# Two short runs of dummy matmuls taken out of a decoder layer on one core

## The reference

```
f1 = swiglu(rms_norm(x, ffn1_pre_g), ffn1_w_gate, ffn1_w_up, ffn1_w_down)
x = x + 0.5 * rms_norm(f1, ffn1_post_g)
m = token_mixer(rms_norm(x, mix_pre_g), w_in, b_forget, sb_group_g, fox_group_g, w_out)
x = x + rms_norm(m, mix_post_g)
f2 = swiglu(rms_norm(x, ffn2_pre_g), ffn2_w_gate, ffn2_w_up, ffn2_w_down)
x = x + 0.5 * rms_norm(f2, ffn2_post_g)
gate = sigmoid(rms_norm(x, ple_pre_g) @ w_ple_gate)
x = x + rms_norm(gate * (p @ w_ple_proj), ple_post_g)
```

## Time and profile before

| | us |
|---|---|
| median of 3 runs | 1078.36 |
| the runs | 1078.16 to 1078.60 |
| the profiled execution, own time | 1078.24 |
| its span, first to last instruction | 1076.5 |
| TensorE's matmuls busy (PE) | 1062.5 (99%) |
| VectorE busy (DVE) | 618.6 (57%) |
| ScalarE busy (ACT) | 510.1 (47%) |
| GpSimd busy (POOL) | 9.9 (1%) |
| granted TensorE clock, mean | 1.000 |

### The profile page before, as it was taken

One profiled execution on the slowest core, in us unless ns is written; L12 is line 12 of the kernel. 1 busy time (PEld: TensorE's weight loads), 2 busy tenths in 40 slices (PEclk: granted clock), 3 DMA queues, 4 the chain that ended last, 5 costly groups with the idle time before them and its releaser, 6 DMA issues.

```text
span 1076.5 us, 15222 instructions
## 1 busy us (share of the span) xinstructions
PE 1062.5 (99%) x4966; PEld 887.9 (82%) x4966; DVE 618.6 (57%) x1043; ACT 510.1 (47%) x930; POOL 9.9 (1%) x33
## 2 busy tenths in 40 slices
PE   9999999999999999999998999999999999999997
PEld 7888888888888878888887888888888888888886
DVE  6454445444222689797979889544455445333655
ACT  6433333333222558686869746433333334333645
POOL 1000000000020000000000000000000000000000
PEclk9999999999999999999999999999999999999999
DMA  6333333333333332332312123333333334444002
GB/s 215 90 88 107 97 97 88 105 99 95 94 97 97 79 89 69 79 79 69 83 56 65 55 76 87 100 91 105 97 97 86 109 116 134 152 135 146 1 20 79
DMA packets 100948, 100.24 MB, mean 93 GB/s; under 512 B 7696, under 2 KB 83216, under 8 KB 100912
## 3 DMA queue, kind: packets, MB, share of 16 engines
q1 hardware_dynamic: 100496, 99.48, 31.7%
q10 hardware_dynamic: 416, 0.30, 0.1%
HBM read 94.44 MB, written 2.10 MB: 90 GB/s over the span
## 4 chain that ended last, share of the span: by engine, by line
PE 87%; DVE 6%; ACT 4%; issue 2%; DMA 0%; DVEq 0%; ACTq 0%
PE bank L1425 27%; PE bank L1426 27%; PE bank L1427 27%; PE bank L1737 1%; DVE w_r L931 1%; PE bank L1752 1%; DVE scratch L1323 1%; ACT scratch L669 0%; DVE big L1103 0%; PE bank L1701 0%; DMA gains<-in_gains 0%; ACT scratch L667 0%; DVE big L1100 0%; DVE acc L951 0%; DVE scratch L1094 0%
## 5 line engine op out<-in xcount | busy, mean ns | idle before, releaser
L931 DVE TENSOR_TENSOR w_r<-w_raw,w_r 128x512 fp32r<-128x512 f32 x332 | 225.4, 691 | 380.6 <-ACT w_r L510 374.9
L510 ACT ACTIVATE w_r<-w_raw 128x512 fp32r<-128x512 f32 x332 | 204.4, 628 | 403.8 <-PE bank L1427 400.7
L1425 PE MATMUL bank<-xg,w_r 128*128 128x512 f32 x890 | 349.2, 392 | 0.6 <-DVE scratch L1094 0.6
L1426 PE MATMUL bank<-xg,w_r 128*128 128x512 f32 x890 | 346.6, 389 | 0.0
L1427 PE MATMUL bank<-xg,w_r 128*128 128x512 f32 x890 | 346.5, 389 | 0.0
L1425 PEld LDWEIGHTS bank<-xg,w_r 128*128 128x128 f32 x890 | 167.1, 188 | 36.6 <-issue 1.4
L1427 PEld LDWEIGHTS bank<-xg,w_r 128*128 128x128 f32 x890 | 167.1, 188 | 35.2
L1426 PEld LDWEIGHTS bank<-xg,w_r 128*128 128x128 f32 x890 | 167.1, 188 | 34.5 <-issue 0.7
L1425 PE MATMUL bank<-big,w_r 128*128 (+2 forms) x420 | 163.5, 389 | 0.6 <-DVE big L1108 0.5
L1426 PE MATMUL bank<-big,w_r 128*128 (+2 forms) x420 | 162.6, 387 | 0.0
L1427 PE MATMUL bank<-big,w_r 128*128 (+2 forms) x420 | 162.6, 387 | 0.0
(11 more groups left out here) (168 smaller groups left out, 950.6 us busy)
## 6 DMA issues: line engine op xcount, KB each, us to landing
w_raw<-in_ffn_w_up SPq DMA_DIRECT2D x88, 256.0 KB, 2.8
w_raw<-in_ffn_w_down SPq DMA_DIRECT2D x88, 256.0 KB, 2.7
w_raw<-in_ffn_w_gate SPq DMA_DIRECT2D x87, 256.0 KB, 2.8
w_raw<-in_w_in SPq DMA_DIRECT2D x36, 256.0 KB, 3.1
scratch<-in_w_ple_gate SPq DMA_DIRECT2D x16, 256.0 KB, 3.4
w_raw<-in_w_in SPq DMA_DIRECT2D x24, 128.0 KB, 2.3
big<-big SPq DMA_DIRECT2D x24, 128.0 KB, 2.2
w_raw<-in_w_out SPq DMA_DIRECT2D x8, 256.0 KB, 2.8
```

The source lines that it names most:

```text
L510: act.activation(w_slot(0, slot, 0, 4 * P), w_raw[:, slot, :], ACT.Copy).then_inc(w_hi, 1)
L931: dve.tensor_tensor(w_slot(1, slot, 0, 4 * P), w_raw[:, slot, :], plain(w_slot(0, slot, 0, 4 * P)), SUB).then_inc(w_lo, 1)
L1425: pe.matmul(dst, w_hi_ap, m_hi, start=start, stop=False, skip_group_check=True)
L1426: pe.matmul(dst, w_lo_ap, m_hi, start=False, stop=False, skip_group_check=True)
```

## The change

The calls of `keep_busy` at the end of the first down projection and behind the output projection are left out. The 14 calls at the start of the program stay.

```diff
@@ -1573,8 +1573,6 @@
                 sum_halves(n, (bank[4], bank[7]))
                 if f == 1:
                     p_project(1)
-                if f == 0:
-                    keep_busy(8, bank[5])
 
             def p_project(r):
                 half, b = divmod(r, TB)
@@ -1858,7 +1856,6 @@
                 first_halves(i)
                 second_halves(i)
             sum_halves(N_MIX_POST, (bank[0], bank[3]))
-            keep_busy(8, bank[1])
             up(1, 2)
             down(1)
```

## The result

The changed kernel takes 1080.86 us (median of 19 runs, 1079.36 to 1082.36), the kernel before, in 19 runs of the same measurement, 1078.40 us (1077.98 to 1079.05). The ratio is 1.0020 with a 95% interval of 1.0014 to 1.0026: 2.5 us slower. The profiled execution took 1080.86 us over a span of 1078.0, with a mean granted clock of 0.996.

A forecast was written before the change was run, and what follows sets the result against it. The prediction took TensorE's stream of products at 2.4 GHz (87% of the chain) as the bound; terms 0 + 0 + 0 on 1078.24 us gave 1078.24, stated as 1078.3, range for 8 in 10 1077.7 to 1080.0.

The forecast's parts named there:

- The direct term: At both places, 1.95 us less TensorE work minus 1.95 us more waiting for ScalarE's xg: 0.
- The chain not shortened: ScalarE and VectorE pieces from row sums to xg gain nothing without dummies beside them: 0.1 us at most, taken as 0.
- waking free: First products behind each longer stand cost nothing extra: taken as 0, upper bound 0.1 us per place.
- The clock at 0: TensorE's granted clock stays at 2.4 GHz through and behind both stands of about 2.3 us: 0 us.
- The price of a fall: Cost if the clock drops to 1.2 GHz behind a stand: 1.4 us each, 2.6 us as upper end.
- The rival with two falls: Clock falls in both gaps between row sums and next first product: 2.8 us together, 1081.1 us; chance 0.09.
- that with one: Clock falls in one of the two gaps, or in some executions only: 1.4 us, 1079.7 us; chance 0.07.
- the 1.74 us outside the span: Time around the profiled execution's 1076.5 us span, included unchanged in the forecast's base of 1078.24 us.

The follow-up runs named there:

- 2 calls: Kernel before with 2 calls of the dummy product instead of 8 at both places: 1079.87 us against 1078.51.
- second trace of the changed kernel: Profiled execution of a repeat run of the changed kernel, same change against the kernel before: 1081.00 us against 1078.41; this trace's span 1079.5.
- the program's length restored: Changed kernel with 8 calls of the dummy product added behind TensorE's last transposes, where nothing waits for them: 1079.81 us; kernel before 1078.76.
- 4 calls: Kernel before with 4 calls of the dummy product instead of 8 at both places: 1078.52 us against 1078.41.
- two stands close together: Kernel before with 2 calls instead of 8 at both places, issued mid-stand after a wait for the first half's exponential: 1079.35 us against 1078.41.

## Why the prediction was wrong

- **The direct term** was right: 16 matmuls less, 1.8 us more of waiting at each place, stands of 2.32 and 2.31 us against 2.32 and 2.30, and the first product at 371.28 in both kernels. The prediction wrote 1.95 us more of waiting, but the first dummy starts 0.16 us before the last row sum ends, so it is 1.95 - 0.16; the sum of 0 isn't touched.
- **The chain not shortened, waking free:** right. L531 and L988 take as long as before, and the first pair behind the stand 0.47 us as in the earlier trace rows.
- **The clock at 0** is the step that failed: "I take 0 for the clock". The runs show 1.4 us in the span's median instead, one or two paid falls of 1.1 to 1.4 us per execution. The 0 rested on two readings. The first took the one stand of 2.33 us at full clock as a sample of what such a stand does; the kernel before falls there in most executions. The second said that a fall there would show in the times, which agree. It doesn't show, since that stage has slack: 1.6 us lost by TensorE leave 0.38 us at the start of the second SwiGLU block. I had priced a fall by the stage behind the row sums and used the price for another stage. The last of the earlier trace rows could have told: the 20 matmuls stand in front of a further wait of 0.51 us, which a slower TensorE eats first.
- **The price of a fall** was right in size: 1.4 us from the program's start, against 1.24 us in the trace, 1.1 to 1.4 us between the profiled executions with and without a fall, and steps of 1.4 us in the executions with 2 calls.
- **The rival with two falls** (1081.1 us, given 9%) and that with one (1079.7, 7%) are the mechanism, together: all 19 executions have at least one step, 7 are in the upper group. The argument for them, that only one gap of equal length was on record, was in the text and should have weighed more. The second trace of the changed kernel has a fall behind all three stands. The passage of the Trainium skill's page "TensorE: Matmul & The Clock Gate", section "A second HAM failure mode: psum-queue depth-cycling", on short stands that make the clock swing, which I held to be not borne out by the trace of before, agrees with that trace in kind: the clock falls and comes back behind stands of 2.30 to 2.33 us. The page tells of frequent stands, and here single ones far apart were enough.
- **A term was missing:** the sum carried the 1.74 us outside the span over unchanged, and the changed kernel takes 2.41 us there in the median, 0.67 us more. With the 1.4 us that the median span grew (1076.7 in the later comparisons, to 1078.1) that makes 2.1 of the 2.5 us; medians of groups in steps don't add up exactly. Means do: the change costs 2.30 us (1080.76 against 1078.46), of which 0.57 lie outside the span (2.31 against 1.74) and so 1.7 inside it, which fits the 26 paid falls of the 19 executions at 1.1 to 1.4 us each. With the program's length restored the loss is 1.05 us (1079.81 against 1078.76). The clock alone would thus still have been a loss, and the time outside the span made it larger.

## What to carry to other kernels

A trace shows the clock of one execution; whether it falls behind a stand varies from one to the next, so a stand at full clock in one trace is no proof that stands of that length are free. Look at the mean clock of many executions, and price a fall in the stage that follows: where TensorE is the bound, 3.4 us at 1.2 GHz cost 1.1 to 1.4 us here, where it has slack, some 0.3 us. Dummy products in a wait that is there anyway cost nothing here and needn't fill it: 4 calls did what 8 do, 2 did not.

## What the runs showed of the hardware that was not expected

- The clock fell within 0.1 us of the stand's end (three times) or up to 1.4 us behind it, with TensorE busy again, never early in the stand. In each of the 13 falls in the middle of the profiled executions it then stayed at 1.2 GHz for 3.4 us, as from 372.7 to 376.1 in the first.
- With two stands close together, 0.58 and 1.03 us at the one place, 7 of 11 executions were up by one or two steps of the size of a fall.
- The program of TensorE that is shorter by 32 matmuls with their weight loads, with 20 packets instead of 21 in the instruction queue, took up to 1.2 us more outside the span than one shorter by 16, though nothing in the span shows it.
